# Mixture-of-experts stage of a two-block model: expert bias from four row groups, weight tiles as transfers of 1 MB, and indirect transfers that skip empty places

## The chip, the cores and the metric

The kernel runs on one core of a Trainium2 chip. The metric is device microseconds of one execution, the median of three runs. In what follows PE is TensorE, DVE is VectorE, ACT is ScalarE, POOL is GpSimd, and SP is the sync engine that issues most DMAs.

## The reference

Two transformer-like blocks over 512 tokens of width 1024, all in fp32. The change touches only the expert part at the end of the first block:

```python
logits = xt @ w_router + b_router
top_v, top_e = lax.top_k(logits, TOP_K)               # 4 of 32 experts for each of 512 tokens
weights = jax.nn.softmax(top_v, axis=-1)
...
def expert_block(args):
    tok, e = args
    hcat = x_pad[tok] @ w1[e] + b1[e]                 # 1024 -> 2048
    x_glu = jnp.minimum(hcat[:, ::2], SWIGLU_LIMIT)
    x_lin = jnp.clip(hcat[:, 1::2], -SWIGLU_LIMIT, SWIGLU_LIMIT)
    act = x_glu * jax.nn.sigmoid(SWIGLU_ALPHA * x_glu) * (x_lin + 1.0)
    return act @ w2[e] + b2[e]                        # 1024 -> 1024
```

Every expert has 8 MB of `w1` and 4 MB of `w2`. The 512 tokens choose four experts each, so 2048 rows are really computed.

## The kernel before

**Routing.** The router stage builds, for each expert, 128 places. `token_of_slot` (`x_at`) says which token stands in a place, `y_row_of_slot` (`y_at`) to which row of the DRAM tensor `y_rows` its result goes (row 4 × token + choice). 32 experts × 128 places are 4096, for 2048 rows of work. A place without a token fetches row 0 and stores to one of 128 spare rows at the end of `y_rows`.

**The experts.** `experts_pass` runs all 32 experts in one loop, written out for five engines (`on_sync`, `on_gpsimd`, `on_tensor`, `on_scalar`, `on_vector`), each in a fixed program order with semaphores between them. (A second copy of the pass, for experts with more than 128 tokens, is only run if one has them.) On PE a turn of expert e is: `up` (96 matmuls: 8 slices of 128 input features × 4 banks × 3 products of rounded and remainder parts), the transposes of the next gathered rows (8, `turn_inputs`), `down` of expert e−1 (48 matmuls), the transposes of expert e's hidden values (8 on `lin`), and then `up` of e+1. `up` begins with the bias: for each of four banks one matmul of a selecting column (`b1_pick`) on `b1_parts`, a tile of 36 partitions: rows 0 to 3 hold the four quarters of the bias rounded, rows 32 to 35 their remainders.

**Weights.** The weight ring has 8 places of 1 MB, called halves here (128 partitions × 2048 fp32). An expert uses 12 halves, 8 for `up` and 4 for `down`. SP loads them as tiles of 2 MB, so two halves at a time; `loaded` has a semaphore for each of four tiles. The number of halves used up is `used`, which PE raises; half q goes where half q−8 was. ACT rounds each half to fp32r (L2473, `round_half`) into a ring of four, so it also waits until half q−4 is used; DVE subtracts to get the remainder (L2534, `split_half`), and PE waits for that (`w_split`). After `up`, DVE reads the banks (L2594, L2596), splits half 11, forms the product (L2606), splits the next gathered rows (L2543), and only then splits the first halves of the next `up`.

The waits that the change concerns:

```python
def load_tile(t, o, src, dims):
    q, slot, _, _ = t.half(o)
    if not (t.first and prefetched):
        sp.wait_ge(used, q + (free0 - 6))         # both halves q-8 and q-7 are used
```

**Rows.** POOL issues an indirect DMA for each expert to fetch its rows (`gather`, three experts ahead) and one to store its results (`scatter`).

**Around it.** The first gather is waited for at the stage's start. At its end SP reads `y_rows` back in four parts, one for each choice, and DVE sums them.

Of the kernel before, what the change touches and what calls it, by code (L numbers as in the profile page):

```python
# [29 lines left out]
P = 128  # L30
# [21 lines left out]
def constants():  # L52
# [14 lines left out]

    c["b1_pick"] = ((i[:, None] % 32 == np.arange(4)[None, :]) & (i[:, None] < 36)).astype(np.float32)

# [4 lines left out]
    for l in range(6):  # L74
# [8 lines left out]
CONST_W = [("ident", P), ("flip", P), ("head_sum", P), ("ones", P), ("cum_f", P), ("cum_b", P), ("before", P),  # L83
           ("slot_iota", P), ("b1_pick", 4)]

# [223 lines left out]
def build(nc, a, out):  # L309
    ctx = ExitStack()  # L310
    with ctx:
# [1670 lines left out]
        h_rows = nc.dram_tensor("h_rows", (T, D), F32).ap()  # L1982
        y_rows = nc.dram_tensor("y_rows", (TOPK * T + P, D), F32).ap()
        router = ctx.enter_context(ExitStack())
# [17 lines left out]
        def read_tables(nc, dve):  # L2002

            nc.vector.tensor_copy(x_at[:, :], ps[:, 5, 0:E])
            nc.vector.tensor_scalar(spare[:, :], ps[:, 5, E:2 * E], 0.0, col("token"), ALU.is_ge, ALU.mult)
            dve.drain()
            nc.vector.scalar_tensor_tensor(spare[:, :], ps[:, 5, E:2 * E], float(TOPK * T), spare[:, :], ALU.add, ALU.add)
            dve.drain()
            nc.vector.scalar_tensor_tensor(y_at[:, :], ps[:, 5, 0:E], float(TOPK), spare[:, :], ALU.mult, ALU.add)

        with stage(*NORM, "tables_loaded", "first_rounded", "hf_even", "hf_odd", "h_turned", "h_ready", "h_stored", "turned_logits", "logits_copied",
# [11 lines left out]
            @block.sync  # L2023
            def _(sp):
                sp.dma_start(w_router[:, :, :], a["w_router"][0].rearrange("(k p) e -> p k e", p=P)).then_inc(tables_loaded, 16)
                sp.dma_start(b2_sb[:, :], a["b2"][0]).then_inc(tables_loaded, 16)
                for t in range(TT):
                    sp.wait_ge(h_ready, t + 1)
                    sp.dma_start(h_rows[P * t:P * t + P, :], h_out[:, t, :]).then_inc(h_stored, 16)
                ring.settle(sp)  # L2030
                sp.wait_ge(h_stored, 16 * TT)

            @block.tensor
# [168 lines left out]
        experts = ctx.enter_context(ExitStack())  # L2202
        x_rows = sb(experts, "gathered_rows", [P, 2, D])
        xg_hi = sb(experts, "gathered_hi", [P, DK, P], F32R)
        xg_lo = sb(experts, "gathered_lo", [P, DK, P], F32R)
        b1_pick = sb(experts, "b1_pick", [36, 4], F32R)
        b1_full = sb(experts, "b1_full", [4, 512])
        b1_parts = sb(experts, "b1_parts", [36, 512], F32R)
        glu = sb(experts, "glu", [P, DFF])
# [9 lines left out]
        def experts_pass(rounds, prefetched, sems, joined):  # L2219
# [82 lines left out]
            def on_sync(sp):  # L2302
                def load_b1(e):
                    row = b1[e:e + 1, :] if isinstance(e, int) else b1[bass.ds(e, 1), :]
                    sp.dma_start(b1_full[:, :], row.rearrange("e (n f) -> (e n) f", n=4)).then_inc(b1_loaded, 16)

                def load_tile(t, o, src, dims):
                    q, slot, _, _ = t.half(o)
                    if not (t.first and prefetched):
                        sp.wait_ge(used, q + (free0 - 6))  # L2310
                    room = ring.buf[:, 2 * slot:2 * slot + 2, :].rearrange("p s n -> p (s n)").rearrange("p (a b) -> p a b", a=dims[0])
                    sp.dma_start(room, src).then_inc(loaded[slot], 16)

                def prologue(t):
                    if rounds:
                        sp.wait_ge(used, t.q0 + free0)
                    load_b1(0)
                    if prefetched:
                        for o in (0, 2):
                            sp.nop().then_inc(loaded[t.half(o)[1]], 16)  # L2320

# [18 lines left out]
            def on_gpsimd(pool):  # L2340

                def gather(r, e):
                    pool.wait_ge(x_turned, r * E + e + 1)
                    nc.gpsimd.indirect_dma_start(x_rows[:, e % 2, :], None, h_rows,
                                                 bass.IndirectOffsetOnAxis(x_at[:, e:e + 1], 0)).then_inc(gathered[e % 2], 16)

                def scatter(r, e):
                    pool.wait_ge(y_read, r * E + e + 2)
                    nc.gpsimd.indirect_dma_start(y_rows, bass.IndirectOffsetOnAxis(y_at[:, e:e + 1], 0), y_out[:, e % 2, :], None)\  # L2349
                        .then_inc(y_stored[e % 2], 16)  # L2350
# [28 lines left out]
            def on_tensor(pe):  # L2379
# [88 lines left out]
            def on_scalar(act):  # L2468
                def round_half(t, o):
                    h = t.half(o)  # L2470
                    act.wait_ge(loaded[h[1]], t.landed(o))
                    act.wait_ge(used, h[0] + (free0 - 3))
                    nc.scalar.activation(hi_half(h), full_half(h), ACT.Copy).then_inc(w_rounded, 1)  # L2473

                def round_b1(n):
                    act.wait_ge(b1_loaded, n * 16 + 16)
                    nc.scalar.activation(b1_parts[0:4, :], b1_full[:, :], ACT.Copy).then_inc(b1_rounded, 1)

# [44 lines left out]
                with when_needed(act):  # L2523
                    nc.scalar.activation(b1_pick[:, :], K["b1_pick"][0:36, 0:4], ACT.Copy)
                    nc.scalar.activation(b1_parts[:, :], const[0:36, 0:512], ACT.Copy, scale=0.0)
                    act.drain()
                    act.nop().then_inc(y_read, 1)
                    each_turn(act, prologue, turn)

            def on_vector(dve):  # L2530
# [5 lines left out]
                def split_b1(n):  # L2536
                    dve.wait_ge(b1_rounded, n + 1)
                    nc.vector.tensor_tensor(b1_parts[32:36, :], b1_full[:, :], b1_parts[0:4, :], ALU.subtract).then_inc(b1_ready, 1)

# [88 lines left out]
        first_tiles = ring.units[block2_at:block2_at + 2]  # L2628
        with stage(*pass_sems, *[f"late_{n}" for n in pass_sems], *[f"late_tiles_loaded{n}" for n in range(4)], "joined",
                   "first_rows", "second_rows", "third_rows", *[f"last_rows{t}" for t in range(TT)], "second_added", "x_ready", "tiles_loaded") as (  # L2630
                block, *sems):
            n = len(pass_sems)
            joined, first_rows, second_rows, third_rows, *last_rows, second_added, x_ready, tiles_loaded = sems[2 * n + 4:]
            of_pass = experts_pass(0, True, sems[0:n] + ring.loaded[0:4], joined)
            of_rounds = experts_pass(T // P - 1, False, sems[n:2 * n + 4], joined)
            halves_used = sems[n - 1]

            @block.sync
            def _(sp):
                of_pass[0](sp)  # L2640
                of_rounds[0](sp)
                rows_of = lambda j: y_rows[0:TOPK * T, :].rearrange("(t p j) d -> j p t d", p=P, j=TOPK)[j]
                sp.wait_ge(y_stored[0], 16 * (E // 2 - 1))
# [984 lines left out]
```

## Time and profile before

| | |
|---|---|
| median of 3 runs | 3086.32 us (3083.18 to 3089.13) |
| the profiled execution | 3090.46 us, span 3088.7 us |
| granted TensorE clock, mean | 0.970 |
| PE busy | 2902.1 us (94% of the span) |
| DVE busy | 2114.9 us (68%) |
| ACT busy | 1589.6 us (51%) |
| POOL busy | 277.6 us (9%) |
| DMA | 607.97 MB, mean 197 GB/s |

The expert stage takes from about 614 to 1856 us of the span. A busy PE is not yet a PE at its peak, since matmuls overlap; starts of matmuls, one to the next, say more. A row of the timeline gives the start, how long the merged group lasts from its first start to its last end, the engine, the line, and at the end in brackets the idle time ahead of it and who ended it.

### The profile page before, as it was taken

Reading aid. Unit: us, or ns where it says so; the run is one execution under the profiler, and the core shown is the slowest. Engines: PE = TensorE matmul, PEld = TensorE weight load, DVE = VectorE, ACT = ScalarE, POOL = GpSimd, SP = SyncE. Lnnn points to the kernel's source line nnn. Section 1 sums busy time; section 2 is a strip of 40 time slices with the busy share of each in tenths; the row PEclk is TensorE's granted clock in tenths of the full one; section 3 lists DMA queues with packets and bytes.
Section 4 is the critical chain, followed back from the end, with each engine's and each line's share of the span. In section 5 each row is a group of like instructions: output and inputs, shape, how many; then the busy total and the mean of one; then the engine's idle time right before and its main releaser. Section 6 shows DMA issues by size and latency. Waiting matters only on the chain. (4 is left out here: it accounts for less than half of the span.)

```text
span 3088.7 us, 46215 instructions
## 1 busy us (share of the span) xinstructions
PE 2902.1 (94%) x18522; PEld 2323.3 (75%) x18522; DVE 2114.9 (68%) x2177; ACT 1589.6 (51%) x1770; POOL 277.6 (9%) x225
## 2 busy tenths in 40 slices
PE   5999999789999999999999968799799999899999
PEld 4777777568777878887888856689677887678877
DVE  6577744558989999998989985566455455466642
ACT  3556532347777777777777745222345463333321
POOL 0110110001111111111111000244000000000000
PEclk9999999879999999999999988999899999999999
DMA  6333343269999999999999983100222222323321
GB/s 249 125 92 102 107 132 122 78 240 370 372 369 367 371 372 369 367 375 369 377 374 372 363 304 105 42 4 4 69 77 61 76 80 86 109 82 96 96 82 69
DMA packets 217388, 607.97 MB, mean 197 GB/s; under 512 B 10792, under 2 KB 118312, under 8 KB 183440
## 3 DMA queue, kind: packets, MB, share of 16 engines
q1 hardware_dynamic: 202496, 554.88, 49.1%
q0 software_dynamic: 14592, 50.36, 4.8%
q8 instruction: 113, 1.85, 0.3%
q10 hardware_dynamic: 144, 0.53, 0.1%
q14 instruction: 43, 0.35, 0.0%
HBM read 582.63 MB, written 23.10 MB: 196 GB/s over the span
## 5 line engine op out<-in xcount | busy, mean ns | idle before, releaser
L2534 DVE TENSOR_TENSOR weight_ring_part<-weight_ring,weight_ring_part 128x2048 fp32r<-128x2048 f32 x380 | 852.2, 2284 | 113.4 <-ACT weight_ring_part L2473 113.4
L2473 ACT ACTIVATE weight_ring_part<-weight_ring 128x2048 fp32r<-128x2048 f32 x380 | 713.2, 1915 | 261.6 <-PE ps L193 133.7
L193 PE MATMUL ps<-weight_ring_part 128*128 128x512 f32 x1456 | 576.8, 396 | 0.0
L189 PE MATMUL ps<-weight_ring_part,gathered_hi 128*128 128x512 f32 x1024 | 409.6, 400 | 0.0
L293 DVE TENSOR_TENSOR weight_ring_part<-weight_ring,weight_ring_part 128x2048 fp32r<-128x2048 f32 x111 | 253.1, 2281 | 226.3 <-ACT weight_ring_part L290 224.6
L193 PE MATMUL ps<-weight_ring_part,gathered_hi 128*128 128x512 f32 x1024 | 406.1, 397 | 0.0
L192 PE MATMUL ps<-weight_ring_part,gathered_lo 128*128 128x512 f32 x1024 | 406.0, 396 | 0.0
L189 PE MATMUL ps<-h1T_hi,weight_ring_part 128*128 128x512 f32 x872 | 356.4, 409 | 3.1 <-DVE weight_ring_part L293 1.7
L192 PE MATMUL ps<-h1T_hi,weight_ring_part 128*128 128x512 f32 x872 | 344.6, 395 | 0.0
L193 PEld LDWEIGHTS ps<-weight_ring_part 128*128 128x128 f32 x1456 | 274.6, 189 | 68.1
L290 ACT ACTIVATE weight_ring_part<-weight_ring 128x2048 fp32r<-128x2048 f32 x111 | 211.1, 1902 | 131.3 <-PE ps L193 103.4
L189 PEld LDWEIGHTS ps<-weight_ring_part,gathered_hi 128*128 128x128 f32 x1024 | 194.0, 189 | 56.8 <-issue 8.6
L193 PEld LDWEIGHTS ps<-weight_ring_part,gathered_hi 128*128 128x128 f32 x1024 | 193.8, 189 | 45.9
L192 PEld LDWEIGHTS ps<-weight_ring_part,gathered_lo 128*128 128x128 f32 x1024 | 194.0, 190 | 44.7
L189 PE MATMUL ps<-weight_ring_part,hidden_hi 128*128 128x512 f32 x512 | 207.4, 405 | 10.0 <-DVE hidden_lo L2581 7.1
L192 PE MATMUL ps<-weight_ring_part,hidden_lo 128*128 128x512 f32 x512 | 203.1, 397 | 0.0
L193 PE MATMUL ps<-weight_ring_part,hidden_hi 128*128 128x512 f32 x512 | 202.5, 396 | 0.0
L189 PEld LDWEIGHTS ps<-h1T_hi,weight_ring_part 128*128 128x128 f32 x872 | 164.5, 189 | 46.6 <-issue 9.2
L192 PEld LDWEIGHTS ps<-h1T_hi,weight_ring_part 128*128 128x128 f32 x872 | 164.3, 188 | 34.9
L2349 POOL DMA_INDIRECT y_rows<-expert_out,y_row_of_slot x32 | 88.1, 2754 | 1025.7 <-ACT expert_out L2489 1025.7
L189 PE MATMUL ps<-hT_hi,weight_ring_part 128*128 128x512 f32 x408 | 171.0, 419 | 2.1 <-PEq L345 1.5
L192 PE MATMUL ps<-hT_hi,weight_ring_part 128*128 128x512 f32 x408 | 162.1, 397 | 0.0
(496 smaller groups left out, 4341.4 us busy)
## 6 DMA issues: line engine op xcount, KB each, us to landing
weight_ring<-in_w SPq DMA_DIRECT2D x190, 2048.0 KB, 9.2
weight_ring<-in_w_in SPq DMA_DIRECT2D x58, 1024.0 KB, 5.4
weight_ring<-in_w_ffn_up SPq DMA_DIRECT2D x44, 512.0 KB, 4.7
weight_ring<-in_w_ffn_down SPq DMA_DIRECT2D x11, 1024.0 KB, 4.9
mod_tile<-in_w_ada POOLq DMA_DIRECT2D x36, 256.0 KB, 3.2
weight_ring<-in_w_ada SPq DMA_DIRECT2D x8, 1024.0 KB, 13.0
gate_rows<-in_w_ada POOLq DMA_DIRECT2D x28, 256.0 KB, 3.2
weight_ring<-in_w_branch SPq DMA_DIRECT2D x6, 1024.0 KB, 6.0
```

What stands on the lines that cost most here:

```text
L189: first = nc.tensor.matmul(out, x[0], y[0], start=start, stop=False)
L192: nc.tensor.matmul(out, x[1], y[0], start=False, stop=False)
L193: return nc.tensor.matmul(out, x[0], y[1], start=False, stop=stop)
L290: self.nc.scalar.activation(hi, full, ACT.Copy).then_inc(self.rounded, 1)
L293: self.nc.vector.tensor_tensor(lo, full, hi, ALU.subtract).then_inc(self.split, 1)
L2349: nc.gpsimd.indirect_dma_start(y_rows, bass.IndirectOffsetOnAxis(y_at[:, e:e + 1], 0), y_out[:, e % 2, :], None)\
L2473: nc.scalar.activation(hi_half(h), full_half(h), ACT.Copy).then_inc(w_rounded, 1)
L2534: nc.vector.tensor_tensor(lo_half(h), full_half(h), hi_half(h), ALU.subtract).then_inc(w_split, 1)
```

## The change

Four things are changed.

1. The bias: `b1_full` and `b1_parts` now have 128 partitions, in four groups of 32. Group n holds quarter n of the bias twice, in its rows 0 and 1 (two small loads an expert in place of one); all other rows are zero, set once. `b1_parts` becomes, with one DVE instruction, minus the rounded value in row 0 and the remainder in row 1. Each of the four bias matmuls reads 32 partitions of its own, so each uses a row group of PE of its own.
2. Weight tiles are loaded by halves, 1 MB each, with a semaphore for each of the eight places, and half q waits only for half q−8.
3. Places without a token get a row number beyond the bounds, and the indirect DMAs are told to leave such rows out. The spare rows go; `x_rows` is allocated one stage earlier and zeroed there once by POOL. One DVE instruction of `read_tables` goes.
4. SP waits until ACT has zeroed `b1_full` before it loads the first bias, and with it before its first weight tiles of the stage.

```diff
+    c["b1_pick"] = np.where(i % 32 == 1, 1.0, np.where(i % 32 == 0, -1.0, 0.0)).astype(np.float32)[:, None]
+    c["b1_low"] = (i % 32 == 1).astype(np.float32)[:, None]
...
-            nc.vector.tensor_copy(x_at[:, :], ps[:, 5, 0:E])
-            nc.vector.tensor_scalar(spare[:, :], ps[:, 5, E:2 * E], 0.0, col("token"), ALU.is_ge, ALU.mult)
+            nc.vector.tensor_scalar(spare[:, :], ps[:, 5, E:2 * E], float(TOPK * T), None, ALU.add)
             dve.drain()
-            nc.vector.scalar_tensor_tensor(spare[:, :], ps[:, 5, E:2 * E], float(TOPK * T), spare[:, :], ALU.add, ALU.add)
-            dve.drain()
+            nc.vector.scalar_tensor_tensor(x_at[:, :], spare[:, :], float(1 - TOPK), ps[:, 5, 0:E], ALU.add, ALU.max)
...
-                    sp.dma_start(b1_full[:, :], row.rearrange("e (n f) -> (e n) f", n=4)).then_inc(b1_loaded, 16)
+                    for r in range(2):
+                        sp.dma_start(b1_full[r:P:32, :], row.rearrange("e (n f) -> (e n) f", n=4)).then_inc(b1_loaded, 16)
...
-                    q, slot, _, _ = t.half(o)
-                    if not (t.first and prefetched):
-                        sp.wait_ge(used, q + (free0 - 6))
-                    room = ring.buf[:, 2 * slot:2 * slot + 2, :].rearrange("p s n -> p (s n)").rearrange("p (a b) -> p a b", a=dims[0])
-                    sp.dma_start(room, src).then_inc(loaded[slot], 16)
+                    rows = dims[0] // 2
+                    for part in range(2):
+                        q, slot, half, _ = t.half(o + part)
+                        if not (t.first and prefetched):
+                            sp.wait_ge(used, q + (free0 - 7))
+                        room = full_half((q, slot, half)).rearrange("p (a b) -> p a b", a=rows)
+                        sp.dma_start(room, src[:, rows * part:rows * part + rows, :]).then_inc(loaded[2 * slot + half], 16)
...
+                    sp.wait_ge(b1_rounded, 1)
                     load_b1(0)
...
-                                                 bass.IndirectOffsetOnAxis(x_at[:, e:e + 1], 0)).then_inc(gathered[e % 2], 16)
+                                                 bass.IndirectOffsetOnAxis(x_at[:, e:e + 1], 0), bounds_check=T - 1, oob_is_err=False)\
+                        .then_inc(gathered[e % 2], 16)
...
-                        nc.tensor.matmul(ps[:, n, :], b1_pick[:, n:n + 1].to_broadcast([36, P]), b1_parts[:, :], start=True, stop=False)
+                        rows = slice(32 * n, 32 * n + 32)
+                        nc.tensor.matmul(ps[:, n, :], b1_pick[rows, 0:1].to_broadcast([32, P]), b1_parts[rows, :], start=True, stop=False)
...
-                    nc.vector.tensor_tensor(b1_parts[32:36, :], b1_full[:, :], b1_parts[0:4, :], ALU.subtract).then_inc(b1_ready, 1)
+                    nc.vector.scalar_tensor_tensor(b1_parts[:, :], b1_full[:, :], K["b1_low"], b1_parts[:, :], ALU.mult, ALU.subtract)\
+                        .then_inc(b1_ready, 1)
```

What SP issues for one expert in the loop, before: four `up` tiles, two `down` tiles, one bias load (`ISA` is the wait, `REGISTER_ALU` its value).

```order
L2312 ISA
L2312 DMA weight_ring<-in_w 128x2x2048
L2310 REGISTER_ALU
L2312 ISA
L2312 DMA weight_ring<-in_w 128x4x1024
L2310 REGISTER_ALU
L2312 ISA
L2312 DMA weight_ring<-in_w 128x4x1024
L2334 REGISTER_ALU
L2305 ISA
L2305 DMA b_full<-in_b 4x512
```

The same place after the change: eight and four loads of half the size, each behind a wait of its own, and two bias loads.

```order
L2319 ISA
L2319 DMA weight_ring<-in_w 128x2x1024
L2317 REGISTER_ALU
L2319 ISA
L2319 DMA weight_ring<-in_w 128x2x1024
L2310 ISA
L2310 DMA b_full<-in_b 4x512 x2
```

The bias loads still stand behind all of an expert's weight loads; what moved is that every half now has its own wait.

On ACT, the beginning of the expert stage, before:

```order
L2524 ACTIVATE b_pick<-const 36x4
L2525 ACTIVATE b_parts<-const 36x512
L2477 ACTIVATE b_parts<-b_full 4x512
L2482 ACTIVATE gathered_hi<-ps 128x512 x2
L2473 ACTIVATE weight_ring_part<-weight_ring 128x2048 x8
```

And after:

```order
L2536 ACTIVATE b_full<-const 128x512
L2537 ACTIVATE b_pick<-const 128x1
L2489 ACTIVATE b_parts<-b_full 128x512
L2494 ACTIVATE gathered_hi<-ps 128x512 x2
L2485 ACTIVATE weight_ring_part<-weight_ring 128x2048 x8
```

The tile that is zeroed is now `b_full`, and it comes first, because SP waits for it; every rounding of the bias covers 128 partitions by 512 where it covered 4 by 512. On PE no row moves.

## Rows read from the trace of the kernel before

**Rows 1.** Windows: 29 of the 32 experts.

```profile
core 0: us, PE busy (x) PEld busy (x) DVE busy (x) ACT busy (x) POOL busy (x), PEclk, DMA share, GB/s
711.34:1777.37 1066.03, 1063.10 (x4758) 852.48 (x4757) 970.75 (x667) 783.00 (x581) 135.24 (x57) 1.00 0.96 371
```

**Rows 2.** Timeline of PE: the bias matmuls of two experts, the first of `up`.

```profile
1521.19 1.19 PE L2390 MATMUL ps<-b_parts,b_pick 36*128 36x512 f32 x4
...
1557.75 1.19 PE L2390 MATMUL ps<-b_parts,b_pick 36*128 36x512 f32 x4
1558.86 0.50 PE L189 MATMUL ps<-weight_ring_part,gathered_hi 128*128 128x512 f32 x1
1559.20 0.39 PE L192 MATMUL ps<-weight_ring_part,gathered_lo 128*128 128x512 f32 x1
1559.43 0.39 PE L193 MATMUL ps<-weight_ring_part,gathered_hi 128*128 128x512 f32 x1
```

**Rows 3.** Waits, longest first, from 711.34 to 1777.37: total us, times, longest.

```profile
ACT weight_ring_part L2473 <- DMA weight_ring<-in_w: 119.1, 59, 4.7
PEld ps L189 <- DVE weight_ring_part L2534: 9.7, 18, 1.5
```

**Rows 4.** The DMA view of the same stretch.

```profile
q1 hardware_dynamic: 62406, 365.14, 88.2%
q0 software_dynamic: 8208, 29.89, 7.9%
...
weight_ring<-in_w SPq DMA_DIRECT2D x174, 2048.0 KB, 9.3
```

**Rows 5.** Durations of the bias matmuls by line, ns min/median/max.

```profile
L2390 PE MATMUL ps<-b_parts,b_pick x128: 383/394/792, 630.5 to 1778.2; 36*128 36x512 f32 x128
```

**Rows 6.** Timeline of PE: four 64-row matmuls in two row groups (block 1), four 32-row ones in one.

```profile
186.33 1.13 PE L1266 MATMUL ps<-xn_tok 64*128 64x512 f32 x4
...
657.48 1.98 PE L2423 MATMUL ps<-xn_tok 32*128 32x512 f32 x4
```

**Rows 7.** Timeline: the first bias matmuls of the stage, at half clock.

```profile
630.49 2.07 PE L2390 MATMUL ps<-b_parts,b_pick 36*128 36x512 f32 x4
632.49 0.79 PE L189 MATMUL ps<-weight_ring_part,gathered_hi 128*128 128x512 f32 x1
```

**Rows 8.** Timeline of DVE and PE: the split awaited at an `up`, two experts.

```profile
856.11 8.89 DVE L2534 TENSOR_TENSOR weight_ring_part<-weight_ring,weight_ring_part 128x2048 fp32r<-128x2048 f32 x4
859.62 0.50 PE L189 MATMUL ps<-weight_ring_part,gathered_hi 128*128 128x512 f32 x1
...
1005.76 8.88 DVE L2534 TENSOR_TENSOR weight_ring_part<-weight_ring,weight_ring_part 128x2048 fp32r<-128x2048 f32 x4
1008.22 0.50 PE L189 MATMUL ps<-weight_ring_part,gathered_hi 128*128 128x512 f32 x1
```

**Rows 9.** Windows: full flow in the expert stage, its slowest stretch, and 1 MB transfers.

```profile
1007.00:1014.00 7.00, 7.00 (x31) 5.40 (x30) 7.00 (x4) 6.02 (x6) 3.29 (x2) 1.00 0.87 311
1022.00:1034.00 12.00, 12.00 (x57) 9.84 (x56) 9.43 (x5) 7.96 (x5) 0.00 (x0) 1.00 1.03 407
...
5.00:15.00 10.00, 0.00 (x0) 0.00 (x0) 5.67 (x3) 0.00 (x0) 0.00 (x0) 1.00 1.02 426
```

**Rows 10.** DMA issues of the page: 1 MB tiles, us from issue to landing.

```profile
weight_ring<-in_w_in SPq DMA_DIRECT2D x58, 1024.0 KB, 5.4
```

**Rows 11.** Timeline of SP: the issue of one weight tile.

```profile
895.46 0.37 SPq L2312 DMA_DIRECT2D weight_ring<-in_w  x1
```

**Rows 12.** Timeline: the first gather, and what waits for it.

```profile
615.24 1.01 POOL L2344 DMA_INDIRECT gathered_rows<-h_rows,token_of_slot  x1 [170.40 <-POOLq L2374]
...
624.89 1.97 PE L2383 MATMUL ps<-const,gathered_rows 128*128 128x128 f32 x8 [3.32 <-DMA gathered_rows<-h_rows,token_of_slot]
```

**Rows 13.** Timeline of DVE in the stage's last microseconds.

```profile
1833.19 4.87 DVE L2690 SCALAR_TENSOR_TENSOR xn_tok<-weight_ring,soft,xn_tok 128x1024 f32<-128x1024 f32 x4 [4.45 <-DMA weight_ring<-y_rows]
...
1843.49 1.28 DVE L2702 SCALAR_TENSOR_TENSOR weight_ring<-weight_ring,soft,gate_rows 128x1024 f32<-128x1024 f32 x1 [0.39 <-DMA weight_ring<-y_rows]
```

More of the change, by code:

```diff
@@ L83 @@
 CONST_W = [("ident", P), ("flip", P), ("head_sum", P), ("ones", P), ("cum_f", P), ("cum_b", P), ("before", P),
-           ("slot_iota", P), ("b1_pick", 4)]
+           ("slot_iota", P), ("b1_pick", 1), ("b1_low", 1)]
 def t5_bucket_np(dist):
@@ L1982, in build @@
         h_rows = nc.dram_tensor("h_rows", (T, D), F32).ap()
-        y_rows = nc.dram_tensor("y_rows", (TOPK * T + P, D), F32).ap()
+        x_rows = sb(moe, "gathered_rows", [P, 2, D])
+        y_rows = nc.dram_tensor("y_rows", (TOPK * T, D), F32).ap()
         router = ctx.enter_context(ExitStack())
@@ L2031, in _ @@
                 sp.wait_ge(h_stored, 16 * TT)
+            @block.gpsimd
+            def _(pool):
+                nc.gpsimd.memset(x_rows[:, :, :], 0.0)
+                pool.drain()
             @block.tensor
@@ L2202, in build @@
         experts = ctx.enter_context(ExitStack())
-        x_rows = sb(experts, "gathered_rows", [P, 2, D])
         xg_hi = sb(experts, "gathered_hi", [P, DK, P], F32R)
         xg_lo = sb(experts, "gathered_lo", [P, DK, P], F32R)
-        b1_pick = sb(experts, "b1_pick", [36, 4], F32R)
-        b1_full = sb(experts, "b1_full", [4, 512])
-        b1_parts = sb(experts, "b1_parts", [36, 512], F32R)
+        b1_pick = sb(experts, "b1_pick", [P, 1], F32R)
+        b1_full = sb(experts, "b1_full", [P, 512])
+        b1_parts = sb(experts, "b1_parts", [P, 512], F32R)
         glu = sb(experts, "glu", [P, DFF])
@@ L2316, in prologue @@
                         sp.wait_ge(used, t.q0 + free0)
+                    sp.wait_ge(b1_rounded, 1)
                     load_b1(0)
                     if prefetched:
-                        for o in (0, 2):
-                            sp.nop().then_inc(loaded[t.half(o)[1]], 16)
+                        for o in range(4):
+                            _, slot, half, _ = t.half(o)
+                            sp.nop().then_inc(loaded[2 * slot + half], 16)
                 def turn(t):
@@ L2470, in round_half @@
                     h = t.half(o)
-                    act.wait_ge(loaded[h[1]], t.landed(o))
+                    act.wait_ge(loaded[2 * h[1] + h[2]], t.landed(o))
                     act.wait_ge(used, h[0] + (free0 - 3))
@@ L2475, in round_b1 @@
                 def round_b1(n):
-                    act.wait_ge(b1_loaded, n * 16 + 16)
-                    nc.scalar.activation(b1_parts[0:4, :], b1_full[:, :], ACT.Copy).then_inc(b1_rounded, 1)
+                    act.wait_ge(b1_loaded, n * 32 + 32)
+                    nc.scalar.activation(b1_parts[:, :], b1_full[:, :], ACT.Copy).then_inc(b1_rounded, 1)
                 def round_inputs(n):
@@ L2523, in on_scalar @@
                 with when_needed(act):
-                    nc.scalar.activation(b1_pick[:, :], K["b1_pick"][0:36, 0:4], ACT.Copy)
-                    nc.scalar.activation(b1_parts[:, :], const[0:36, 0:512], ACT.Copy, scale=0.0)
+                    nc.scalar.activation(b1_full[:, :], const[:, 0:512], ACT.Copy, scale=0.0).then_inc(b1_rounded, 1)
+                    nc.scalar.activation(b1_pick[:, :], K["b1_pick"], ACT.Copy)
                     act.drain()
@@ L2628, in build @@
         first_tiles = ring.units[block2_at:block2_at + 2]
-        with stage(*pass_sems, *[f"late_{n}" for n in pass_sems], *[f"late_tiles_loaded{n}" for n in range(4)], "joined",
+        with stage(*pass_sems, *[f"late_{n}" for n in pass_sems], *[f"late_tiles_loaded{n}" for n in range(8)], "joined",
                    "first_rows", "second_rows", "third_rows", *[f"last_rows{t}" for t in range(TT)], "second_added", "x_ready", "tiles_loaded") as (
@@ L2632, in build @@
             n = len(pass_sems)
-            joined, first_rows, second_rows, third_rows, *last_rows, second_added, x_ready, tiles_loaded = sems[2 * n + 4:]
-            of_pass = experts_pass(0, True, sems[0:n] + ring.loaded[0:4], joined)
-            of_rounds = experts_pass(T // P - 1, False, sems[n:2 * n + 4], joined)
+            joined, first_rows, second_rows, third_rows, *last_rows, second_added, x_ready, tiles_loaded = sems[2 * n + 8:]
+            of_pass = experts_pass(0, True, sems[0:n] + ring.loaded[0:8], joined)
+            of_rounds = experts_pass(T // P - 1, False, sems[n:2 * n + 8], joined)
             halves_used = sems[n - 1]
@@ L2641, in _ @@
                 of_rounds[0](sp)
-                rows_of = lambda j: y_rows[0:TOPK * T, :].rearrange("(t p j) d -> j p t d", p=P, j=TOPK)[j]
+                rows_of = lambda j: y_rows[:, :].rearrange("(t p j) d -> j p t d", p=P, j=TOPK)[j]
                 sp.wait_ge(y_stored[0], 16 * (E // 2 - 1))
```

6 lines of the change are left out of this document (3 added, 3 removed).

## The prediction

> **What bounds the kernel now.** I first cut the expert stage into windows [rows 1]. From 711 to 1777 us, 29 experts, PE is busy 1063.10 of 1066.03 us at full clock, and the DMA engines show a share of 0.96. Both look full, so the shares alone do not say which one sets the pace. The starts of matmuls do: in an expert without a wait they follow each other every 0.23 us (1559.20, 1559.43) through `up` and `down`, and from one expert's bias to the next such an expert takes 1557.75 − 1521.19 = 36.56 us [rows 2], all of it PE's own work. The 29 experts took 1066.03 / 29 = 36.76 each. So PE stood for waits only 29 × 0.20 = 5.9 us in all. The list of waits agrees: ACT waits 119.1 us for weights, but PE waits only 9.7 us for DVE's splits [rows 3]; most of ACT's lateness is absorbed on the way. And the DMA engines have room: in full flow they move 407 GB/s, over the stretch only 371, and in some stretches 311 [rows 1, 9], because a 2 MB tile has to wait until two halves are free.
>
> So **PE's own instructions set the pace**, with DVE's chain and the weights close behind.
>
> **The bias, the largest term.** Now: four matmuls in 1.19 us from first start to last end, the last of them 0.39 long [rows 2, 5], so the last starts 0.80 after the first, and the first matmul of `up` starts 1558.86 − 1557.75 = 1.11 after it. After: the four sit in four different row groups of PE. Does PE run these side by side? Block 1 has the nearest case: four fp32 matmuls of 512 columns, two of rows 0 to 63 and two of rows 64 to 127 (the two maps of a head), take 1.13 us; four of 32 rows that all lie in one row group take 1.98 us at the same clock [rows 6]. Two go in the time of one. I take it that four groups behave as two do, with about 0.02 us for all the starts. Then 0.80 becomes 0.02: **0.78 us an expert**. Bounds: nothing at all if four groups do not overlap; if they go as two pairs, two of the three steps go, 0.8 × 2/3 = 0.5. A change of the array's division costs time before and after; I count it unchanged, since the 36-row matmuls also differ from the 128-row ones around them, and the 0.31 us that remain (1.11 − 0.80) already hold that.
>
> [...]
>
> That PE is done earlier helps only if the split of the first `up` half is there. In a good expert it is: the split starts at 856.11, takes 8.89 / 4 = 2.22, ends at 858.33, and `up` starts at 859.62, 1.29 later; in a late one it ends at 1007.98 and `up` starts at 1008.22 [rows 8]. About 0.2 is the least, so a late expert can give back nothing of the 0.78. I counted this gap in the timelines for experts 2 to 31: 15 of the 30 have 1.0 us or more, the others 0.2 to 0.9. If nothing else changed, the saving would be 0.78 in the 15 and 2.5 us over all the others together: 14 us and not 30 × 0.78 = 23.4. The first two experts run their bias at half clock, 632.49 − 630.49 = 2.00 us [rows 7]; three steps of 0.43 to 0.59 go, 1.4 us each, 2.8 together.
>
> **The transfers.** What makes the late experts late is ACT's 59 waits for weights [rows 3], two for each expert, which push DVE's reading of the banks and with it the split. Before, a tile is issued when half q−7 is used and lands 9.3 us later [rows 4]; ACT wants its first half when q−4 is used, three halves or 3 × 12 × 0.232 = 8.4 us after issue. That is just too little. After, half q is issued when q−8 is used, four halves or 11.1 us ahead, and tiles of 1 MB landed in 5.4 us elsewhere in this kernel [rows 10]. Even if two are in flight it is in time. The load falls too: an expert now moves 365.14 / 29 = 12.6 MB of weights and 29.89 / 29 = 1.03 MB of rows [rows 4]; half of the places are empty, so 0.5 MB of it goes, and 13.1 MB at 407 GB/s is 32.2 us, against 35.8 us of PE. So I expect ACT's waits for weights to nearly vanish, the whole 23.4 of the bias to be had, and the 5.9 us of waits with it. SP issues 14 DMAs an expert in place of 7; one takes it 0.37 us [rows 11], 14 of them 5.2 of 36 us, and nothing else stands on SP. POOL's rows stay (two DMAs an expert, idle otherwise).
>
> [...]
>
> **The small edits.** The bias loads go from one to two of 8 KB, which stand where the one stood, long before they are wanted. Rounding and splitting the bias cover 128 partitions where they covered 4; the 512 elements along a partition stay, and I count the time as unchanged. DVE's margin in a good expert covers it, and if that were gone, each 0.1 us more would cost 3 us over 32 experts. The memset on POOL lies in a stage where POOL idled 170 us [rows 12]. One DVE instruction and one drain fewer in `read_tables`, on the way to the stage's barrier: 0.3 us (0 to 0.5). SP's wait for ACT at the beginning delays the first weight tiles by about one ACT instruction; nobody wants them before PE has used a first half, and that is behind the wait for the first gather. This gather was issued at 615.24, and PE waited 3.32 us for it [rows 12]; with half the rows and less beside it I take 1.5 of it back (0 to 3.3). At the stage's end DVE waits 4.45 and then 0.39 us for rows that stand behind the last two scatters [rows 13]; with half the rows in them I take 0.7 (0 to 2).
>
> **The sum.** 23.4 + 2.8 + 5.9 + 0.3 + 1.5 + 0.7 = 34.6 us. The profiled execution had 3090.46 us for a span of 3088.7; it lies 4.1 above the median of the runs, 0.13%, and nothing in it calls for a correction, so the sum goes off the median. 3086.3 − 34.6 = **3051.7 us**.
>
> **The rivals.**
>
> *The waits stay.* The four matmuls run side by side, but ACT still waits for weights as before (the sum of transfers, not their size, was late, or the split is late for a reason on DVE itself, which is busy 970.75 of 1066.03 us). Then the bias brings 14 + 2.8, and of the rest 2.5: 3086.3 − 19.3 = 3067. For it: the split's margin in a good expert is 1.29 − 0.2 = 1.1 us, only 0.3 more than the saving needs. Chance 0.14.
>
> *Four row groups do not overlap.* The bias costs what it did; the transfers bring 5.9 + 2.5: 3078. Half an overlap (two pairs) would give 3086.3 − 30 × 0.5 − 1.8 − 8.4 = 3061. For it: only two groups have been seen side by side. Against it: those two overlap wholly. Chance 0.08 for none, 0.06 for half.
>
> *Nothing to be measured.* The bias doesn't overlap and the waits only move: within 6 us of before. Chance 0.05.
>
> *Slower: the pieces of 1 MB do not keep up.* PE now needs 35.8 us for 12 halves, so the DMA engines must deliver 13.1 MB in that time, 366 GB/s; under this the pace is theirs. At the 311 GB/s of the slowest stretch [rows 9] an expert takes 42.1 us, 5.3 more than now, over 32 experts 170 us: 3256. It decides against the change from 13.1 / 36.76 = 356 GB/s down. For it: twice the transfers, each with an end of its own, since 1 MB lands in 5.4 us of which its bytes at 407 GB/s are only 2.6. Against it: these ends overlap with the next transfer, as at the start of this kernel. [...] Chance 0.04.
>
> *More than forecast.* The gather and the scatter of each expert also slow the queue for other reasons than their bytes, and both ends of the stage give their bounds: up to 5 us more, 3046. Chance 0.08.
>
> **How the numbers follow.** The forecast case has 0.55. A difference of 0.2% (6 us) is about what a measurement of this kernel can tell from none. Faster by more: 0.55 + 0.14 + 0.08 + 0.06 + 0.08 = 0.91; a little of it may be lost in that margin, so 0.9. The same 0.06, slower 0.04. The range from 3043 to 3070 holds the forecast, the larger gain, the waits that stay and the half overlap, together 0.83.
>
> **What the profile after would show.** The four bias matmuls as one group of about 0.4 us, and `up` about 0.33 us after its start, not 1.11. From one bias to the next 35.8 us in nearly all experts. ACT's wait for weights under 20 us in all. Bytes on q0 about half. The DMA rate of the stretch near 366 GB/s. I am wrong if the bias group still lasts over 0.8 us, if the split of the first half becomes the wait at every `up`, or if ACT waits for weights as long as before.

## The result, and the profile after

The kernel after takes **3054.68 us** (median of 4 runs, 3053.95 to 3056.35) against 3084.75 us before (4 runs, 3081.99 to 3089.13): a ratio of 0.9896, 95% interval 0.9883 to 0.9908. That is 30 to 32 us less; 3051.7 was forecast, in a range of 3043 to 3070. (The first table had three of the four runs of before.) The profiled executions differ by more, 3088.7 − 3052.2 = 36.5 us of span. Of this 3.6 us stand already at the router's last steps (the same DVE instruction starts at 598.5 before and at 594.9 after), ahead of the expert stage; the code up to there is the same, and in the other kernels below that instruction starts anywhere from 595.0 to 600.0. Behind the stage the code is the same in all kernels here, too, and that rest took from 1231.4 to 1238.0 us (1232.5 before, 1234.8 after). These differences are chance. So I compare stretches of the stage and not whole spans.

The window of the 29 experts between the third bias and the last, as in [rows 1]:

```profile
core 0: us, PE busy (x) PEld busy (x) DVE busy (x) ACT busy (x) POOL busy (x), PEclk, DMA share, GB/s
699.90:1740.40 1040.50, 1040.50 (x4757) 840.07 (x4756) 972.25 (x668) 792.98 (x581) 119.11 (x57) 1.00 0.97 366
```

1066.03 us have become 1040.50: 25.5 less, 35.88 an expert in place of 36.76, and all 29 are equal to 0.01 us. PE has no gap at all. The DMA share has risen from 0.96 to 0.97 although the rate fell from 371 to 366 GB/s, so the share does not measure how near the DMA engines are to their limit.

The list of waits of that stretch has no wait of ACT for weights any more (119.1 us in [rows 3]), and none of PE for a split:

```profile
POOL y_rows L2359 <- ACT expert_out L2501: 928.8, 29, 49.6
ACT weight_ring_part L2485 <- PE ps L194: 190.1, 232, 0.9
ACT glu L2526 <- DVE glu L2607: 57.5, 58, 1.4
DVE weight_ring_part L2546 <- ACT weight_ring_part L2485: 34.3, 87, 0.5
DVE b_parts L2550 <- ACT b_parts L2489: 29.0, 29, 1.0
```

ACT now waits for PE to use up a half, 232 times and never over 0.9 us: the pace comes from PE and is handed on.

The timeline of PE at a bias, which answers to [rows 2]:

```profile
1022.81 0.51 PE L2402 MATMUL ps<-b_parts,b_pick 32*128 32x512 f32 x4
1023.25 0.51 PE L190 MATMUL ps<-weight_ring_part,gathered_hi 128*128 128x512 f32 x1
1023.59 0.39 PE L193 MATMUL ps<-weight_ring_part,gathered_lo 128*128 128x512 f32 x1
```

Four matmuls take 0.51 us from first start to last end, where they took 1.19. `up` starts 0.44 after the first, not 1.11 and not the 0.33 that I had expected. By line, all four last as long as the first one did before:

```profile
L2402 PE MATMUL ps<-b_parts,b_pick x128: 488/496/1410, 620.5 to 1740.4; 32*128 32x512 f32 x128
```

The DMA view, against [rows 4]: the rows' bytes are halved, the number of packets is the same.

```profile
q1 hardware_dynamic: 65424, 365.40, 92.7%
q0 software_dynamic: 8208, 15.05, 3.8%
...
weight_ring<-in_w SPq DMA_DIRECT2D x348, 1024.0 KB, 7.0
```

The start of the stage, against [rows 12]: 617.57 − 611.40 = 6.17 us from the first gather's issue to its transposes, where there were 9.65, and no wait.

```profile
611.40 1.08 POOL L2353 DMA_INDIRECT gathered_rows<-h_rows,token_of_slot  x1 [42.32 <-POOLq L2385]
...
617.57 1.97 PE L2394 MATMUL ps<-const,gathered_rows 128*128 128x128 f32 x8
```

And its end, against [rows 13]: DVE waits 2.54 us for the last rows where it waited 0.39. Counted from the last bias, it is still at them sooner, after 1804.74 − 1740.41 = 64.3 us and not 1843.49 − 1777.37 = 66.1.

```profile
1804.74 1.28 DVE L2715 SCALAR_TENSOR_TENSOR weight_ring<-weight_ring,soft,gate_rows 128x1024 f32<-128x1024 f32 x1 [2.54 <-DMA weight_ring<-y_rows]
```

### The profile page after: what moved, and what is told of

It reads as the page before. It is cut to its first block and busy times, and to the rows that moved or that the text cites. A ratio compares the mean times of both kernels' runs of the same rounds, so it can differ in the third digit from the quotient of the medians.

```text
span 3052.2 us, 47043 instructions
## 1 busy us (share of the span) xinstructions
PE 2873.2 (94%) x18522; PEld 2306.5 (76%) x18522; DVE 2115.0 (69%) x2176; ACT 1600.2 (52%) x1770; POOL 264.6 (9%) x226
## 5 line engine op out<-in xcount | busy, mean ns | idle before, releaser
L2485 ACT ACTIVATE weight_ring_part<-weight_ring 128x2048 fp32r<-128x2048 f32 x380 | 722.6, 1919 | 223.7 <-PE ps L194 223.7
L291 ACT ACTIVATE weight_ring_part<-weight_ring 128x2048 fp32r<-128x2048 f32 x111 | 211.1, 1902 | 132.5 <-PE ps L194 104.5
L193 PEld LDWEIGHTS ps<-h1T_hi,weight_ring_part 128*128 128x128 f32 x872 | 165.3, 190 | 35.1
L2359 POOL DMA_INDIRECT y_rows<-expert_out,y_row_of_slot x32 | 71.6, 2238 | 1011.1 <-ACT expert_out L2501 1011.1
```

The costliest lines, as they stand in the source:

```text
L193: nc.tensor.matmul(out, x[1], y[0], start=False, stop=False)
L291: self.nc.scalar.activation(hi, full, ACT.Copy).then_inc(self.rounded, 1)
```

## The experiments

### Each part alone, and all but the transfers

The first three kernels are the kernel before with one part of the change, the fourth is the kernel after without one. For the bias alone the lines of `b1_*` are as in the diff above, with SP's wait for ACT, which is item 4 of the change; the tiles stay at 2 MB:

```diff
-                        nc.tensor.matmul(ps[:, n, :], b1_pick[:, n:n + 1].to_broadcast([36, P]), b1_parts[:, :], start=True, stop=False)
+                        rows = slice(32 * n, 32 * n + 32)
+                        nc.tensor.matmul(ps[:, n, :], b1_pick[rows, 0:1].to_broadcast([32, P]), b1_parts[rows, :], start=True, stop=False)
```

> The kernel before with the bias change alone: four row groups, tiles of 2 MB, all places fetched and stored. Theory (PE sets the pace, but an expert whose weights came late can't use the saving): the bias block falls from 1.11 to about 0.44 us in every expert, but only some 15 of 30 experts get shorter by it; 10 to 16 us less than before, about 3070 to 3075, and ACT's waits for weights stay near 120 us or grow, since PE now asks for weights faster. Rival (the margin at the split is not real, the pace is PE's alone): 32 x 0.67 = 21 us and more, 3063 or less.

3073.73 us, ratio 0.9962 (0.9949 to 0.9974). The 29 experts take 1056.22 us: 9.8 less than before, where 29 × 0.67 = 19.4 would be there to have. The shortest takes 35.88, 24 of the 29 take over 0.1 more. Its waits:

```profile
ACT weight_ring_part L2477 <- DMA weight_ring<-in_w: 126.7, 60, 4.4
...
PEld ps L190 <- DVE weight_ring_part L2538: 22.2, 33, 1.5
```

PE's weight loads now wait 22.2 us for splits, not 9.7. Half of the saving has turned into this wait, as the theory said. (The profiled execution is the fastest of the six, 3066.95 us; behind the stage it took 1231.4 us, the least of all.)

The transfers alone (before, with the new `load_tile` and eight semaphores):

```diff
-                    if not (t.first and prefetched):
-                        sp.wait_ge(used, q + (free0 - 6))
+                    for part in range(2):
+                        ...
+                            sp.wait_ge(used, q + (free0 - 7))
```

> The kernel before with the transfers of 1 MB alone. Theory: ACT's waits for weights vanish nearly wholly, every expert takes 36.56 us, and 5 to 9 us go, 3076 to 3080. Rival (the lateness was a matter of bytes, that is of the rows): the waits stay at over 80 us and the time at 3084.

3082.26 us, ratio 0.9986 (0.9976 to 0.9995). No wait of ACT for weights is left, and each expert takes 36.55 us:

```profile
708.32:1768.37 1060.05, 1060.05 (x4758) 853.76 (x4757) 975.44 (x668) 790.96 (x581) 133.95 (x57) 1.00 0.95 373
```

6.0 us of the loop, which are the 5.9 that PE had waited. The median is 4.6 us under that of before in the same series, a little less than the 5 to 9 that I had expected.

The rows alone:

```diff
-                                                 bass.IndirectOffsetOnAxis(x_at[:, e:e + 1], 0)).then_inc(gathered[e % 2], 16)
+                                                 bass.IndirectOffsetOnAxis(x_at[:, e:e + 1], 0), bounds_check=T - 1, oob_is_err=False)\
+                        .then_inc(gathered[e % 2], 16)
...
```

> The kernel before with the places without a token left out of the indirect transfers, alone. Theory: half of the bytes of the rows go, but ACT's waits for weights fall only in part (to 60 to 100 us); 2 to 6 us less, mostly at the stage's first gather, 3079 to 3083. Rival (bytes were the cause): waits under 20 us, every expert at 36.56 us, 8 us less or more.

3085.24 us, ratio 0.9995 (0.9985 to 1.0005): nothing that can be measured, where I had expected 2 to 6 us. From the first gather's issue to its transposes it is 8.69 us, 1.0 less than before. The 29 experts take 1066.03 us, as before, and ACT's wait is the same but for 6 us:

```profile
ACT weight_ring_part L2478 <- DMA weight_ring<-in_w: 113.2, 59, 4.2
```

That the two sums agree to the last digit is chance: 16 experts are over 0.1 us late here and 13 before, and two kernels further down, which run the same loop as before, took 1063.35 and 1063.72 us for it. With 2 MB tiles the loop is not known more closely than some 3 us.

Bias and rows together, tiles of 2 MB (the kernel after with the old `load_tile`):

> The kernel after with tiles of 2 MB again, so bias and rows changed. Theory (size of the transfers decides): ACT waits for weights again, over 60 us in all, experts of uneven length, 8 to 15 us slower than after: 3063 to 3070. Rival (bytes decide): as after, 3055, all experts at 35.88 us.

3068.06 us, ratio to before 0.9938 (0.9922 to 0.9955). The 29 experts take 1053.23 us, 3.0 less than with the bias alone (1056.22), and 12.7 more than the kernel after. The 3.0 are no more than the scatter just named and can't be put down to the rows. ACT waits longer than ever:

```profile
ACT weight_ring_part L2482 <- DMA weight_ring<-in_w: 140.2, 76, 4.3
```

So it was mostly the size of the transfers that decided, and not the bytes.

### All but the rows

The kernel after with all places fetched and stored:

> The kernel after with all places fetched and stored again, so bias and transfers of 1 MB changed. Theory (size of the transfers decides): experts still take 35.88 us, only the wait for the first gather comes back; 1 to 4 us slower than after, 3056 to 3059. Rival (bytes decide): ACT waits for weights in many experts, 8 us slower or more, 3063 and up.

3053.02 us, ratio 0.9893 (0.9876 to 0.9909); the kernel after had 0.9896. Every expert takes 35.88 us, at a rate of 380 GB/s:

```profile
701.26:1741.77 1040.51, 1040.51 (x4757) 840.00 (x4756) 972.07 (x668) 792.19 (x581) 132.40 (x57) 1.00 0.97 380
```

The theory of the size was right for the loop, but the wait for the first gather did not come back, though I had expected it to (3056 to 3059): it is 620.08 − 613.82 = 6.26 us from its issue to the transposes. That wait did not go with the rows, then. The last two experiments return to it.

### Four groups, one group, no division

```diff
-                        rows = slice(32 * n, 32 * n + 32)
+                        rows = slice(0, 32)
```

> The kernel after, but all four bias matmuls read the first 32 partitions, so all lie in one row group and the last three banks get the first bank's bias: the output is not the reference's. The instructions and their number are the same. Theory (the gain is that the four run side by side): the block from the first bias matmul to up goes from 0.44 back to about 1.1 us, all experts 0.67 longer, 36.55, about 21 us slower than after, 3076. Rival (32 rows are quicker in themselves, or the group's place matters little): within 5 us of after.

3078.42 us, ratio 0.9981 (0.9972 to 0.9991), 24 to 26 us over the kernel after, of which the 29 experts have 20.5. (The kernel leaves out three quarters of the bias, since all four banks get the first bank's; its instructions are the same.) An expert takes 36.59, and the block is back:

```profile
1142.15 1.19 PE L2402 MATMUL ps<-b_parts,b_pick 32*128 32x512 f32 x4
1143.27 0.50 PE L190 MATMUL ps<-weight_ring_part,gathered_hi 128*128 128x512 f32 x1
```

Only the partitions differ from the kernel after. So it is the place in different row groups that lets the matmuls run side by side, and not their having 32 rows.

```diff
-                        nc.tensor.matmul(ps[:, n, :], b1_pick[rows, 0:1].to_broadcast([32, P]), b1_parts[rows, :], start=True, stop=False)
+                        nc.tensor.matmul(ps[:, n, :], b1_pick[:, n:n + 1].to_broadcast([P, P]), b1_parts[:, :], start=True, stop=False)
```

> The kernel after, but each bias matmul covers all 128 partitions with a selecting column of its own, so the array is never divided. Theory (a change of the array's division costs about 0.1 us going in, in the matmul whose weights can't be loaded ahead, and 0.1 coming out): transposes, four matmuls and up follow at 0.11 and 0.23 us each, 1.04 us from the last transpose to up against 0.64 after and 1.31 before; 0.4 us an expert slower than after, 3067. Rival (division is free): as four matmuls one behind another in one row group, 3076.

3067.22 us, ratio 0.9942 (0.9925 to 0.9958); 36.18 us an expert.

```profile
1135.45 0.71 PE L2471 MATMUL ps<-const,lin 128*128 128x128 f32 x5
1135.92 1.17 PE L2401 MATMUL ps<-b_parts,b_pick 128*128 128x512 f32 x4
1136.93 0.39 PE L190 MATMUL ps<-weight_ring_part,gathered_hi 128*128 128x512 f32 x1
1137.16 0.39 PE L193 MATMUL ps<-weight_ring_part,gathered_lo 128*128 128x512 f32 x1
```

The division is not free: 36.59 − 36.18 = 0.41 us an expert, which four groups earn back (35.88). Where it shows is in these rows and those of the kernel after. Undivided, the second product of `up` follows the first after 0.23 us, divided after 0.34 (1023.25 to 1023.59), and the last bias matmul is followed by `up` after 0.23 here (four starts in 1.01 us), but after 0.43 there. A third part lies ahead of the block: the first bias matmul starts 0.20 us after the last transpose in the kernel after, and 0.03 here. So the steps are longer on both sides of a change (0.20 against 0.03, 0.43 against 0.23). The weight loads differ there too: undivided, the one of `up`'s first product starts 0.23 us ahead of its matmul (1136.70 and 1136.93), divided it starts with it, at 1023.25.

### Issue or landing

```diff
-                            sp.wait_ge(used, q + (free0 - 7))
+                            sp.wait_ge(used, q + (free0 - 6 - part))
```

> The kernel after with transfers of 1 MB that are issued only when a pair of halves is free, at the times at which the 2 MB tiles were. Theory A (what was late was the landing of a 2 MB tile as one whole): the first half of a pair lands in about 5 to 7 us, before the 8.4 us that there are; no waits, as after, 3055. Theory B (what was late was the issue): ACT waits for weights as with 2 MB tiles, 5 us slower than after or more.

3055.08 us, ratio 0.9906 (0.9889 to 0.9922), and each expert at 35.88: as the kernel after, theory A. The transfers of 1 MB were issued when the tiles of 2 MB had been, and landed in 7.2 us (median), inside the 8.4 that there are:

```profile
weight_ring<-in_w SPq DMA_DIRECT2D x349, 1024.0 KB, 7.2
```

What was late before was that the first half of a tile could only be used once all of the tile had landed, 9.3 us after the issue [rows 4]. The earlier issue, on which I had spent as many words, is worth nothing here.

### The first gather, and a version that is faster

```diff
+                    sp.wait_ge(b1_rounded, 1)
                     load_b1(0)
...
-                    nc.scalar.activation(b1_parts[:, :], const[0:36, 0:512], ACT.Copy, scale=0.0)
+                    nc.scalar.activation(b1_parts[:, :], const[0:36, 0:512], ACT.Copy, scale=0.0).then_inc(b1_rounded, 1)
...
```

> The kernel before with SP's wait for ACT's zeroing alone, ahead of the first bias load and the first weight tiles of the expert stage. Theory (this wait, and not the rows left out, ended PE's 3.3 us of waiting for the first gather: the gather now stands ahead of the weight tiles on the DMA engines): the gather's rows are there some 6.2 us after its issue, not 9.6, and PE waits for them under 0.5 us; 3 us less than before, 3083. Rival (the wait went for another reason, such as the faster bias): 9.6 us and PE's wait of over 3 us stay.

3086.61 us, ratio 1.0003 (0.9993 to 1.0013). The theory fell: 623.09 − 613.67 = 9.42 us from issue to transposes, and PE waited 3.10. The wait did move SP, but not far enough. Before, the bias load stood 615.24 − 614.36 = 0.88 us ahead of the gather's issue, here 0.11. The weight tiles were issued at 614.02, and POOL was not done with the gather's issue before 613.67 + 1.01 = 614.68. In the kernel after that order is turned:

```profile
611.11 1.22 SPq L2310 DMA_DIRECT2D b_full<-in_b  x2
612.64 2.32 SPq L2319 DMA_DIRECT2D weight_ring<-in_w  x4
```

The two bias loads, whose four rows lie 32 partitions apart, hold SP for 1.22 us where the one took 0.27; the first tile goes out at 612.64, and POOL is done at 611.40 + 1.08 = 612.48. To test this, the kernel before with the tiles behind ACT's rounding of the first bias:

```diff
                     load_b1(0)
+                    sp.wait_ge(b1_rounded, 1)
```

> The kernel before with one wait moved in: SP loads the first bias as before, but issues the first two weight tiles of the stage only when ACT has rounded that bias, some 2 us later than before and so behind the first gather's issue instead of ahead of its end. Theory (in the kernel after it was the two strided bias loads, 1.22 us on SP in place of 0.27, that put the weight tiles behind the gather on the DMA engines): from the gather's issue to the transposes 6.2 us, not 9.6, and no wait of PE for the gather; about 3 us less than before. Rival (the order on the DMA engines does not matter): 9.6 us and a wait of over 3 us, as before.

3082.03 us, ratio 0.9986 (0.9976 to 0.9995), with PE's wait gone:

```profile
611.82 1.01 POOL L2345 DMA_INDIRECT gathered_rows<-h_rows,token_of_slot  x1 [171.57 <-POOLq L2375]
...
618.08 1.97 PE L2384 MATMUL ps<-const,gathered_rows 128*128 128x128 f32 x8
```

6.26 us, all places fetched. So the order in which the two are issued made this 3.4 us. In the kernel after it is a by-product: the slower bias loads put the tiles 0.95 us later, and SP's wait some 0.6 to 0.8. The wait alone did not turn the order. Whether the slower loads alone would have, no run shows; by an estimate from these rows the tiles would then go out about 0.5 us after the start of the gather's issue (0.41 ahead of it before, 0.95 later), still before POOL is done.

The last pair: the kernel after unchanged, and one with two edits on DVE. Half 11 is split later in the first turn, and at the stage's end three row groups, not two, are made ready while DVE waits for the last rows.

```diff
-                        if t.first and not rounds:
-                            add_bias(3)
-                        split_half(t, 11)
+                        late = t.first and not rounds
+                        if not late:
+                            split_half(t, 11)
...
                             split_inputs(t.i + 2)
+                        if late:
+                            split_half(t, 11)
+                            add_bias(3)
...
-                for t in range(2):
+                for t in range(3):
                     nc.vector.tensor_tensor(total[:, t, :], total[:, t, :], gate, ALU.mult)
...
-                    if t < 2:
+                    if t < 3:
```

> The kernel after once more, unchanged, for a comparison with the next one on the same chip: 3052 to 3056.

> The kernel after with two edits on DVE. In the first turn, where PE stands 8.8 us for the hidden values with nothing to do, DVE splits half 11 and adds the last output bias only after the products and the next gathered rows: PE's wait should fall by 3.3 to 3.5 us. At the stage's end three of the four row groups, not two, are scaled and added to x while DVE waits for the last rows: 1.3 us less. In all 4.6 us less than after, 3050; the experts between stay at 35.88 us. Rival (the moved split is then late for up of expert 1): the 3.3 us come back as a wait in that expert, 3053.

After again: 3056.10 us (3054.29 to 3058.99), ratio to before 0.9902 (0.9887 to 0.9917). With the edits: **3048.96 us** (3048.39 to 3053.56), ratio 0.9882 (0.9867 to 0.9898). The runs of the two don't overlap, though the intervals do. The wait that the first edit aimed at fell from 8.75 to 5.42 us:

```profile
658.16 1.97 PE L2472 MATMUL ps<-const,lin 128*128 128x128 f32 x8 [5.42 <-DVE gathered_lo L2556]
```

and the loop took 1040.52 us, so the moved split is not late. I expected 4.6 us; the medians give 7.1. The traces give less. From the first gather's transposes to the third bias it is 79.1 us in place of 81.4: only 2.3 of the 3.3 us are left there, at a mean clock of 0.86 in place of 0.88. From the last bias to DVE's last addition of the stage it is 75.6 in place of 76.9, the 1.3 that were expected. So 3.6 us are shown. The rest of the profiled pair's difference, 5.2 us, lies behind the stage, where the code is the same.

## Why the prediction held, and where it was off

**What bounds the kernel.** Right. PE's own work set the pace, and PE waited for 5.9 us in 29 experts; the transfers alone gave 6.0.

**The bias: the term was mis-sized.** Forecast 0.78 us an expert, measured 36.55 − 35.88 = 0.67, so 19.4 us and not 22.6 over 29. That four groups run side by side was right, with starts within 0.02 us. "Then 0.80 becomes 0.02" held. The step that failed was "I count it unchanged": the 0.31 us between the last bias matmul and `up` did not stay, they became 0.43. That is the 0.1 us an expert that was missing. Why it is so was not shown. It may be the same 0.1 us by which the first of the three steps between the four starts was longer than the others (0.33, 0.23, 0.23), standing behind the block instead; that is a guess, and no run tests it.

**The margin at the split.** Right, and the most useful reading in the profile. Counted on the trace of before, the bias alone could give 14 us for 0.78; scaled to 0.67 some 12.5; it gave 9.8. Faster experts are late more often (24 of 29 against 13 of 29), which points the right way, but a loop with 2 MB tiles scatters by as much as the 2.7 us between the two.

**The transfers.** Right in what they do, half wrong in why. "Half q is issued when q−8 is used, four halves or 11.1 us ahead" did not matter; the landing of each half by itself did. The landing took 7.0 us, not the 5.4 of elsewhere, and was in time all the same. Queued one behind another, the transfers of 1 MB ran at 366 to 380 GB/s, the rows' bytes included, with PE as the bound.

**The parts do not add up, and that was the gain.** In the 29 experts the bias alone gives 9.8 us, the transfers alone 6.0, the rows alone 0.0, and all together 25.5. The 9.7 us over the sum are the bias's saving that only timely weights let through: 19.4 were there, and the bias alone got 9.8. The scatter of the loops with 2 MB tiles does not undo this. With 1063.4 us for before, as in the two other traces of its loop, the parts give 7.2 and 3.4 and the whole 22.9, so the excess is 12.3. The medians say the same: 13.2, 4.6 and 1.6 us alone, 30 to 32 together.

**The rows.** I had halved the bytes and counted on it for the load. In the loop they are worth nothing: with all of them fetched it takes 1040.51 us, at 380 GB/s and without a wait of ACT for weights. The 0.3 us of the shorter `read_tables` came as forecast: 0.3 fewer on DVE, 0.2 up to the gather's issue (16.7 us from the router's DVE instruction at 598.5, 16.5 after).

**The first gather.** Forecast 1.5 us, of the rows; measured 9.65 − 6.17 = 3.5, of the order of two DMAs. The rows alone made 1.0, and with the order turned only 0.1 (6.26 with all places, 6.17 with half), so here the term came in for another reason than the one given. "SP's wait for ACT delays the first weight tiles by about one ACT instruction; nobody wants them before" looked only for who waits for the tiles, and not for who shares the DMA engines with them. That the two bias loads "stand where the one stood" was costed at nothing, and together with SP's wait it had this effect.

**The first two experts.** Forecast 2.8 us for the bias at half clock; from the first gather's transposes to the third bias 86.45 us became 82.33, so 4.1. The bias made 1.6 and 1.3 of it, as forecast. The other 1.2 are not those of ACT's waits for weights, 3.2 us in this stretch before and none after. The transfers alone took these waits away and left 86.09, and the kernel with the tiles behind the rounding of the bias kept them and had 84.89. What goes with the time is PE's granted clock, which is at half for parts of this stretch (0.50 from 624.9 to 632.0 before, from 617.6 to 625.0 after); no experiment varied it by itself. The kernels before, after, with the transfers alone, and after again:

```profile
624.89:711.34 86.45, 77.65 (x297) 58.63 (x297) 55.15 (x42) 45.92 (x35) 1.87 (x2) 0.83 0.67 249
...
617.57:699.90 82.33, 73.57 (x300) 56.10 (x299) 57.14 (x44) 45.98 (x35) 1.98 (x2) 0.85 0.75 288
...
622.23:708.32 86.09, 77.30 (x296) 58.53 (x297) 55.14 (x42) 45.89 (x35) 1.87 (x2) 0.83 0.69 261
...
617.63:699.03 81.40, 72.65 (x297) 55.52 (x296) 57.11 (x44) 45.93 (x35) 1.98 (x2) 0.88 0.76 292
```

The second and the last are the same kernel, at mean clocks of 0.85 and 0.88, and differ by 0.9 us. So this term can't be read closer than that.

**The end.** Forecast 0.7 less, for the rows of the last two scatters. From the last bias to DVE's last addition of the stage 78.8 us became 77.0, so 1.8 less. Of this 0.7 are the last expert's bias. The rows do not show in it: from the last scatter's issue to DVE's reading of the last rows it is 8.2 us, before 7.9, and POOL's last scatter took 1.45 us, before 0.95. What made the other 1.1 stays open; the other kernels with 2 MB tiles had 77.2 to 78.3 us.

**The sum** of the stage is 0.2 + 3.5 + 4.1 + 25.5 + 1.8 = 35.1 us in the profiled pair, forecast 34.6. The closeness is in part luck. The loop brought 25.5 where 29.3 was forecast, and the first gather, the first two experts and the end brought 9.4 where 5.0 was, mostly for reasons that the forecast did not have. The profiled execution of before was also a slow one: in the kernel with SP's wait alone, whose gather took 9.4 us too, the same stage was 4.5 us shorter. That goes with the medians, which show 30 to 32 us and not 35.

The rival "the waits stay" was refuted by the list of waits, "groups do not overlap" by one row of the timeline, and "1 MB does not keep up" by the windows.

## What to carry to other kernels

When one engine sets the pace and another stands right behind it, measure the margin of the wait between them in every repetition before counting a saving; two changes can be worth more than their sum (here 25.5 us in the 29 experts, where the parts alone gave 15.8). If a consumer takes a buffer in pieces, give each piece its own transfer and semaphore. And look at which transfers a wait of an engine is queued beside, not only at who waits for it: at this stage's start about a microsecond decided it. In the kernel before with the tiles issued 0.35 us behind the gather's issue, 9.42 us passed up to the transposes; with 1.44 us (613.26 − 611.82), 6.26.

## What the runs showed of the hardware that I had not expected

**Matmuls of other row groups overtake.** At the start of the stage PE has four bias additions on rows 0 to 31 (L2435) ahead of the four bias matmuls (L2402). Three of these start before the last two of those:

```profile
619.47 2.07 PE L2435 MATMUL ps<-xn_tok 32*128 32x512 f32 x2
620.49 0.80 PE L2402 MATMUL ps<-b_parts,b_pick 32*128 32x512 f32 x3
621.34 1.91 PE L2435 MATMUL ps<-xn_tok 32*128 32x512 f32 x2
622.26 1.41 PE L2402 MATMUL ps<-b_parts,b_pick 32*128 32x512 f32 x1
```

The fourth comes after them. Its weight load is the one that has the wait for the bias (at every other `up` that is the first of the four), so it is the one on rows 0 to 31 too. By these records, then, a matmul can start ahead of earlier ones whose row group is not its own.

**A row left out is still a packet.** q0 has 8208 packets in the loop before and after; the skipped rows have become packets under 512 B (3812 in all before, 10337 after; a part of the growth is not of rows, since there are twice as many loads of weights, each with an end of its own; in the kernel with the rows alone they went from 10792 to 14888 over the whole span, by 4096, which are the 2 × 2048 places left out). They cost the DMA engines nearly nothing: the queue's share fell from 7.9% to 3.8%, as its bytes did. POOL's instructions get little shorter: 119 us for 57 of them, before 135, all of it on the scatters.

**A strided load holds the queue.** A load of 8 KB into four rows that are 32 partitions apart takes SP 0.5 to 0.6 us (two in 1.22 at the stage's start, two in 1.08 at the next expert), into four neighbouring ones 0.27.
